# Two softmax packs inside one projection unit, and another order of the sparse branch's packs

## What is computed

```python
for l in range(2):
    P = rmsnorm(x, g_norm[l]) @ w_in[l]
    # A: an indexer scores all keys, each query keeps its top 256, 4 query heads share one key/value head
    # B: 4 heads, causal, with a forgetting term;  C: 4 heads, own chunk + 8 chunks before, learned bias
    # M: 4 heads on 256 memory tokens
    o = concat(branch(P) * silu(gate columns of P) for branch in "ABCM")
    x = x + o @ w_out[l]
y = rmsnorm(x, g_final)
```

## Time and profile before

| What | Value |
|---|---|
| median of the runs | 1696.82 us |
| profiled execution | 1696.26 us, span 1694.5 us |
| TensorE matmul busy | 1673.4 us, 99% |
| TensorE weight load busy | 1044.2 us, 62% |
| VectorE busy | 1011.9 us, 60% |
| ScalarE busy | 651.9 us, 38% |
| GpSimd busy | 238.7 us, 14% |
| granted TensorE clock | full in all 40 slices |

### The profile page before, as it was taken

One profiled execution on the slowest core, in us unless ns is written; L12 is line 12 of the kernel. 1 busy time (PEld: TensorE's weight loads), 2 busy tenths in 40 slices (PEclk: granted clock), 3 DMA queues, 4 the chain that ended last, 5 costly groups with the idle time before them and its releaser, 6 DMA issues.

```text
span 1694.5 us, 27274 instructions
## 1 busy us (share of the span) xinstructions
PE 1673.4 (99%) x9431; PEld 1044.2 (62%) x9431; DVE 1011.9 (60%) x2701; ACT 651.9 (38%) x1529; POOL 238.7 (14%) x452
## 2 busy tenths in 40 slices
PE   9999999999999999999999999999999999999998
PEld 4466666766678655555454666667666786555553
DVE  4747888788877233333245288887888762333322
ACT  3632334333343344544134323343333433445531
POOL 2232321100000100002021423220000001000010
PEclk9999999999999999999999999999999999999999
DMA  9343324122222322113422523241232123221130
GB/s 341 151 169 100 128 94 144 42 78 106 90 87 94 118 74 100 33 50 104 145 105 64 170 79 128 91 144 42 78 110 103 71 97 117 72 94 50 38 105 38
DMA packets 46375, 171.25 MB, mean 101 GB/s; under 512 B 11472, under 2 KB 11952, under 8 KB 43040
## 3 DMA queue, kind: packets, MB, share of 16 engines
q1 hardware_dynamic: 29632, 130.68, 22.9%
q0 software_dynamic: 16608, 38.83, 6.9%
HBM read 141.83 MB, written 30.73 MB: 102 GB/s over the span
## 4 chain that ended last, share of the span: by engine, by line
PE 70%; DVE 23%; issue 3%; ACT 1%; DVEq 1%; DMA 1%; ACTq 0%
PE psX L984 48%; DVE lower L1415 16%; PE psT L897 7%; PE psX L1160 5%; PE psS L1093 5%; DVE work L1662 3%; PE psS L1012 2%; DVE gate L1495 1%; PE psX L897 1%; DMA wring<-in_w 1%; ACT gate L1220 0%; DVE gate L1676 0%; PE psS L897 0%; DVE gate L1694 0%; DVE over L1576 0%
## 5 line engine op out<-in xcount | busy, mean ns | idle before, releaser
L984 PE MATMUL psX<-wring,hT 128*128 128x512 f32 (+2 forms) x2016 | 830.2, 557 | 3.8 <-ACT kv L1268 2.1
L984 PEld LDWEIGHTS psX<-wring,hT 128*128 128x128 f32 x2016 | 366.0, 190 | 330.7 <-issue 322.9
L1415 DVE TENSOR_SCALAR_CACHE_REDUCE lower<-sc,thr 128x640 uint8<-128x640 f32 (+5 forms) x462 | 407.3, 933 | 16.8 <-issue 8.6
L984 PE MATMUL psX<-hT,wring 128*128 128x256 f32 (+1 forms) x1600 | 326.1, 359 | 4.3 <-ACT gate L1305 3.8
L1347 ACT ACTIVATE work<-work,stat 128x256 f32<-128x256 f32 (+7 forms) x288 | 200.1, 695 | 303.6 <-DVEq L1665 301.2
L984 PEld LDWEIGHTS psX<-hT,wring 128*128 128x128 f32 x1600 | 274.8, 190 | 37.0 <-issue 7.3
L1356 ACT COPY work<-psT 128x512 f32<-128x512 f32 (+2 forms) x352 | 156.7, 487 | 313.1 <-PE psT L897 312.1
L897 PEld LDWEIGHTS psT<-con,work 128*128 128x128 f32 x1080 | 121.7, 140 | 69.2 <-issue 60.9
L897 PE MATMUL psT<-con,work 128*128 128x128 f32 x1080 | 158.2, 278 | 0.0
L1662 DVE CUSTOM_DVE_ANT_0 work<-psS,bias 128x640 f32<-128x640 f32 (+7 forms) x120 | 86.2, 718 | 44.1 <-issue 22.4
L1710 POOL DMA_DIRECT2D scratch_oscr<-gate x54 | 30.5, 566 | 402.0 <-DVEq L1696 349.5
(11 more groups left out here) (224 smaller groups left out, 1502.7 us busy)
## 6 DMA issues: line engine op xcount, KB each, us to landing
wring<-in_w SPq DMA_DIRECT2D x16, 2048.0 KB, 9.2
cache<-in_kB SPq DMA_DIRECT2D x16, 512.0 KB, 6.5
cache<-in_vB SPq DMA_DIRECT2D x16, 512.0 KB, 4.0
cache<-in_kC SPq DMA_DIRECT2D x16, 512.0 KB, 5.9
cache<-in_vC SPq DMA_DIRECT2D x16, 512.0 KB, 4.6
scratch_oscr<-gate POOLq DMA_DIRECT2D x54, 128.0 KB, 2.0
hT<-scratch_oscr SPq DMA_DIRECT2D x18, 384.0 KB, 3.1
kv<-in_x SPq DMA_DIRECT2D x9, 512.0 KB, 5.5
```

What stands on the lines that cost most here:

```text
L984: mm = pe.matmul(out, lhs, rhs, start=(kt == 0), stop=(kt == KT - 1))
L1415: v.tensor_scalar(lower[:, at:at + STRIP_L[t]], sc[:, o], thr[:, n:n + 1], 0.0, ALU.is_lt, ALU.add, accum_out=below[:, n:n + 1])
```

## The change

In the units of M1 and A2, when more than one pack waits in the queue, a unit now takes two: its eighths are dealt as 0-1, 1-3, 3-4, V of the pack before, S of the next pack, 4-5, 5-7, 7-8. Sample packs of A, which came after all other packs, are queued one by one behind the first four units of A2 to finish (tile 8, 4, 5, 6), and A2's tiles run in the order 8, 4, 5, 6, 7, 0, 1, 2, 3. No arithmetic, buffer or transfer is added or dropped.

```diff
+A2_ORDER = [ST_, 4, 5, 6, 7, 0, 1, 2, 3]
@@
-    def project(c, t):
-
-        select(pace[0] / 2)
-        emit("Pp", c, t, 0, 2)
-        operands()
-        emit("Pp", c, t, 2, 5)
+    def project(c, t, two_packs=False):
+
+        time = pace[0] / (4 if two_packs else 2)
+        select(time)
+        if two_packs:
+            emit("Pp", c, t, 0, 1)
+            operands()
+            emit("Pp", c, t, 1, 3)
+            odd_heads()
+            select(time)
+            emit("Pp", c, t, 3, 4)
+            settle()
+            advance(queue.pop(0) if queue else None)
+            select(time)
+            emit("Pp", c, t, 4, 5)
+            operands()
+            emit("Pp", c, t, 5, 7)
+        else:
+            emit("Pp", c, t, 0, 2)
+            operands()
+            emit("Pp", c, t, 2, 5)
         odd_heads()
-        select(pace[0] / 2)
+        select(time)
         emit("P", c, t)
@@
-        units += [(c, t) for c in ("M1", "A2") for t in [ST_] + TILES[:NT]]
-        queue = []
+        units += [("M1", t) for t in [ST_] + TILES[:NT]] + [("A2", t) for t in A2_ORDER]
         for c, t in units:
             advance(queue.pop(0) if queue else None)
-            project(c, t)
+            project(c, t, c in ("M1", "A2") and len(queue) > 1)
@@
-        queue += [("A", f"s{j}", j, 1) for j in range(PAIRS)]
+            if c == "A2" and t in A2_ORDER[:PAIRS]:
+                j = A2_ORDER.index(t)
+                queue.append(("A", f"s{j}", j, 1))
```

More of the change, by code:

```diff
@@ L154, in program_order @@
     pace = [0.0]
+    queue = []
     def emit(*s, ahead=0):
@@ L174, in turn_units @@
             if t == ST_:
+                assert not any(p[0] == "M" and is_sample(p) for p in queue)
                 emit("Q", ("A", "s0", 0, 1))
```

## The result

The changed kernel takes 1715.38 us (median of 4 runs, 1712.94 to 1715.87) against 1696.49 us: a ratio of 1.0108, 95% interval 1.0091 to 1.0126. It is 18.9 us slower; 1714 was forecast, range 1699.5 to 1722. The profiled execution took 1712.94 us, span 1711.2, which is 16.7 us more than the profiled one of before.

The account below looks back on a forecast made before the run. TensorE's matmuls were taken as the bound (1673.4 of 1694.5 us). Per layer 3.75 + 1.2 + 4.4 + 0.5 less 1.5 makes 8.4 us, 16.8 in two, plus 0.8 for turns: 1714 us, range 1699.5 to 1722.

Parts of the forecast that it names:

- The bound and what could be saved: TensorE's matmuls bound the kernel; only waits of 1.6 and 1.4 us at the layers' ends, 3.0 us, can be saved.
- M1 2: V in this unit waits 1.2 us for ScalarE's copy of M 0's odd probabilities, behind sample s0's exponential and VectorE.
- M1 4: This unit's first matmul waits 2.1 us for VectorE to read the V just before it, in the same psX buffer.
- M1 5: This unit's start waits 0.65 us, with VectorE's longer ranks and mask of strip 7 but less around it.
- M1 6: This unit's start waits 1.1 us for VectorE, whose gate after an odd tile comes first.
- Starts in A2: Units A2 5, 6, 0 and 3 wait at their starts for VectorE: 0.55 us together per layer.
- V behind one eighth: V waits for ScalarE's copy: 0.21 us in 5 M packs, 0.27 in 10 C and A packs; 3.75 us a layer.
- R of A: With R next to V, it waits behind V's chain and ScalarE's staging: 0.5 us a layer comes back.
- the turns: In layer 0's O units, each of 7 turns of the norm waits about 0.1 us, 0.8 us in all.
- rival C: O units pay more: each of 7 turns may hold TensorE 1 us more, giving 1721 us; chance 0.11.
- The signs of being wrong: V starts right behind its eighth, M1 4 starts unheld, or the matmuls' own busy time grows.
- Rival A: Cover suffices and VectorE's queue has caught up, so only the listed bubbles go: 1693.3 to 1696 us; chance 0.12.

Follow-up runs that it names:

- gt_late: Kernel before, with only the last output units reordered to O0 7, O1 7, O0 8, O1 8: ratio 0.9985, 1693.06 us against 1696.13.
- topk_early: Changed kernel, two-pack units kept, with the top-k search paced so its last piece lies in M1 1, not M1 4: ratio 1.0228, 1734.38 us.
- slots_rounds: Changed kernel with another hand-out of psX's two buffers, and no unit taking two packs while top-k pieces are left: ratio 1.0029 to the kernel before.
- slots: Changed kernel with only the hand-out of psX's two buffers chosen otherwise, steps and order kept: ratio 1.0076 to the kernel before, 1708.46 us.
- cover: Changed kernel with a two-pack unit's eighths dealt as 1, 1, 2, V, 1, 1, 2: ratio 1.0104 to the kernel before.
- cover2: Changed kernel with a two-pack unit's eighths dealt as 1, 2, 2, V, 1, 2: ratio 1.0119 to the kernel before.
- slots_cover2: Changed kernel with another hand-out of psX's buffers and eighths dealt as 1, 2, 2, V, 1, 2: ratio 1.0084 to the kernel before.

## Why the prediction was right, and where it wasn't

- **The bound and what could be saved.** Right: 3.0 us in the earlier trace rows, gone in the changed kernel, worth 3.1 us alone (gt_late). The matmuls' count and the clock didn't move. One reading was wrong: the 159.81 us of the earlier trace rows are the weight load. VectorE's are 96.80, 34% of that stretch and not 56%, which favours the conclusion drawn from it. (The weight load's 62% is also over the "60% or less" given to all else.)
- **M1 2, M1 4, M1 5, M1 6.** Right in place and size: forecast 1.2, 2.1, 0.65 and 1.1 us, the rows show 0.86, 2.24, 0.61 and 1.03. The sum of VectorE's queue from durations of before holds to a few tenths over 10 us. For M1 2 the durations listed add to 9.86 us, not 9.75. The cause is shown by topk_early, where two of the four go and M1 4's halves with the packs unchanged, and slots_rounds, where none is left, agrees. M1 6's is the gate of the odd tile, as forecast.
- **Starts in A2.** The forecast has 0.1, 0.1, 0.25 and 0.1 at A2 5, 6, 0 and 3. The rows show 0.19, 0.32 and 0.45 at the first three, 0.1 to 0.2 more each, and at A2 3 nothing in layer 0 and 0.35 in layer 1.
- **V behind one eighth, 3.75 us a layer.** The term that failed: it was mis-sized. It should be 0.02 us for an M pack and 0.07 for an A pack by the rows, 0.8 us a layer, and slots_rounds has about 0.8 us for all 30 V. (The changed kernel has 16 such V a layer; A 0's was not counted. It starts at 715.07, right at its eighth's end.) The 0.29 us between a copy's end and TensorE's start came from GT's copy, which stands ahead of a unit's first matmul; at V it is 0.09 to 0.10.
- **O0 0.** Missing: 1.11 us a layer. I looked at what each unit's buffer waits for, not at what its operand waits for, although the change's list of tiles moves exactly that.
- **R of A, the turns.** R waits 0.68 us for a forecast 0.5. The turns of layer 0, forecast 0.8 us, wait for nothing; rival C is out.
- **The signs of being wrong.** Two of the three that the prediction named came: V starts within 0.02 to 0.07 us of its eighth, and the matmuls' busy time grew by 5.0 us. The second was meant to point at weight loads next to short groups. slots_rounds deals 11 units a layer in the same short pieces and reads 1675.0 us, 1.6 more than before, so these can't be most of it; what the rest is stays open.
- **The sum.** 1714 against 1715.38 rests partly on luck. V's term was about 3 us a layer too large, M1 2's 0.3 and the turns' 0.8 us too large in all. On the other side stand O0 0 (1.11 us a layer), R, A2's starts and the 5.0 us of added "busy" in both layers, which together come to about as much. Rival A (cover suffices, only the bubbles go) was nearly right on V's cover and wrong on M1. The Trainium skill's rule that independent matmul groups should rotate through PSUM banks ("Perfetto Trace Analysis", section "Optimizing Tensor Performance") pointed at the right place, and slots agrees with it by 5.4 us; that is less than the 8.4 us that the starts waited for `om`, since the next reader stood behind the same backlog.

## What to carry to other kernels

Where TensorE is full, look first at its listed waits and sum those that a change can remove (3.0 us here), and move the one step that waits (gt_late) before rebuilding the schedule around it. When more work is put between two steps of an in-order pipeline, follow the slowest helper engine's queue over the whole distance: its backlog holds whoever comes next, through one buffer or another, and here dealing out cover differently only moved the wait (cover, cover2). For every unit moved, check its operands' last writer as well as its buffer's last reader.

## What the runs showed of the hardware that I had not expected

From the end of ScalarE's copy to V are 0.09 to 0.10 us, and from VectorE's product to the unit that takes its buffer 0.14. The first matmul of a unit that reads what was just written starts later: 0.29 us behind GT's copy and 0.30 behind VectorE's product at O0 0 (718.93 to 719.23). No run here says why.

TensorE's modelled "busy" is not fixed work. The same 9431 matmuls read as 1672.2 us (gt_late) and 1678.4 (changed) at full clock. The 1687.6 us of topk_early are something else: its five stretches at a granted clock of 0.50, 1.7 us each, make 8.5 of the 9.2 us that it has more than the changed kernel.

The clock fell behind waits of 2.01 to 3.24 us. But the length of the one wait doesn't decide it: the clock stayed full behind 2.24 us at M1 4 of the changed kernel and fell behind 2.15 us at M1 5 of slots_cover2. What does is open here. When a schedule makes TensorE wait about 2 us at once, read the granted clock over short stretches behind it; neither the list of waits nor the page's row has this cost.
